# Dilated attention with one softmax for three mixed heads, and experts' further blocks one in a pass

## The reference

```python
for g, (window, r) in enumerate(A_GROUPS):          # (128, 1), (512, 4), (2048, 16)
    o, lse = banded_attention(gather(q), gather(k), gather(v), window // r)
    ...
alpha = jax.nn.softmax(jnp.stack(lses, axis=0), axis=0)
o = jnp.concatenate([outs[g] * alpha[g][..., None] for g in range(3)], axis=2)
return o.reshape(B, T, A_WIDTH) @ w_o
```

## Time and profile before

| | |
|---|---|
| median of 3 runs | 3214.95 us (3212.82 to 3242.93) |
| profiled execution | 3215.8 us, of which the traced span is 3214.1 |
| TensorE busy | 2949.3 us (92%) |
| VectorE busy | 1804.9 us (56%) |
| ScalarE busy | 1418.2 us (44%) |
| GpSimd busy | 537.0 us (17%) |
| DMA | 455.57 MB, mean 142 GB/s |

### The profile page before, as it was taken

How to read it: one execution, slowest core, us unless ns; L and a number is a source line. 1 busy time by engine, 2 the same in 40 slices (tenths; PEclk the granted TensorE clock), 3 DMA queues, 4 the chain that set the end, 5 groups by cost and what they waited for, 6 DMA issues and landing times. The chain is left out here.

```text
span 3214.1 us, 36964 instructions
## 1 busy us (share of the span) xinstructions
PE 2949.3 (92%) x14442; PEld 2357.6 (73%) x14442; DVE 1804.9 (56%) x2210; ACT 1418.2 (44%) x1885; POOL 537.0 (17%) x706
## 2 busy tenths in 40 slices
PE   7978899898998799999999789889999899889998
PEld 4856788787886487777777368678887697678887
DVE  4447745436544498888886344655543327455543
ACT  3324526336223188888786123443332325333332
POOL 0005414124101522232232100000000104000000
PEclk9989999898999799999999889899999999999999
DMA  5210101022652299999997730323322301223331
GB/s 198 60 54 1 60 27 53 27 53 75 213 184 110 96 353 363 364 365 372 375 375 297 280 116 1 92 67 104 106 92 79 95 27 53 73 77 95 92 104 41
DMA packets 277404, 455.57 MB, mean 142 GB/s; under 512 B 24656, under 2 KB 206800, under 8 KB 258160
## 3 DMA queue, kind: packets, MB, share of 16 engines
q1 hardware_dynamic: 250832, 398.43, 35.6%
q0 software_dynamic: 26400, 54.79, 4.7%
HBM read 450.77 MB, written 39.08 MB: 152 GB/s over the span
## 5 line engine op out<-in xcount | busy, mean ns | idle before, releaser
L253 DVE TENSOR_TENSOR weight_part<-weights,weight_part 128x2048 fp32r<-128x2048 f32 (+1 forms) x65 | 148.1, 2279 | 161.7 <-ACT weight_part L242 161.7
L1005 ACT ACTIVATE up_room<-banks,tap_columns 128x512 f32<-128x512 f32 x88 | 68.6, 779 | 315.4 <-PE banks L298 315.4
L293 PE MATMUL banks<-hT_r,weight_part 128*128 128x512 f32 x496 | 200.4, 404 | 4.6 <-PEq L846 2.9
L1046 DVE SCALAR_TENSOR_TENSOR up_room<-banks,tap_columns,up_room 128x511 f32<-128x511 f32 x88 | 66.0, 749 | 240.0 <-ACT up_room L1005 240.0
L242 ACT ACTIVATE weight_part<-weights 128x2048 fp32r<-128x2048 f32 (+1 forms) x65 | 121.7, 1872 | 176.3 <-PE banks L293 170.5
L298 PE MATMUL banks<-hT_r,weight_part 128*128 128x512 f32 x496 | 195.8, 395 | 0.0
L671 POOL TENSOR_SCALAR branch_mean<-branch_mean 128x1 f32<-128x1 f32 x20 | 4.4, 222 | 1129.7 <-ACT up_room L665 750.1
L293 PE MATMUL banks<-hT_r,weight_part_o 128*128 128x512 f32 x432 | 174.7, 404 | 7.1 <-PEq L110 4.2
L253 DVE TENSOR_TENSOR weight_part_o<-weights,weight_part_o 128x2048 fp32r<-128x2048 f32 (+2 forms) x49 | 106.9, 2181 | 127.0 <-ACT weight_part_o L242 127.0
L298 PE MATMUL banks<-hT_r,weight_part_o 128*128 128x512 f32 x432 | 170.9, 396 | 0.0
L297 PE MATMUL banks<-h_low,weight_part_o 128*128 128x512 f32 x432 | 169.8, 393 | 0.0
(11 more groups left out here) (723 smaller groups left out, 8834.9 us busy)
## 6 DMA issues: line engine op xcount, KB each, us to landing
weights<-in_w_e_gate SPq DMA_DIRECT2D x44, 1024.0 KB, 15.8
weights<-in_w_e_up SPq DMA_DIRECT2D x44, 1024.0 KB, 10.8
hT<-in_w_e_down SPq DMA_DIRECT2D x44, 1024.0 KB, 16.9
weights<-in_w_up SPq DMA_DIRECT2D x88, 512.0 KB, 5.1
gate_up<-in_w_e_gate SPq DMA_DIRECT2D x22, 1024.0 KB, 15.7
gate_up<-in_w_e_up SPq DMA_DIRECT2D x22, 1024.0 KB
down<-in_w_e_down SPq DMA_DIRECT2D x22, 1024.0 KB
weights<-in_w_down SPq DMA_DIRECT2D x20, 1024.0 KB, 5.0
```

Source lines behind the costliest of these rows:

```text
L253: c.nc.vector.tensor_tensor(low[:, 0:z], self.raw[n % RAW_SLOTS][:, 0:z], high[:, 0:z].bitcast(F32), ALU.subtract).then_inc(self.low_ready, 1)
L293: ins = c.nc.tensor.matmul(out, lhs[0], rhs[0], start=start, stop=False)
L1005: nc.scalar.activation(a[:, f % 2, v], c.ps[:, 2 * (f % 4) + v], ACT.Identity, scale=conv[:, 2, ch:ch + 1], bias=bias[:, ch:ch + 1]).then_ ...
L1046: nc.vector.scalar_tensor_tensor(a[:, f % 2, v, 1:], c.ps[:, 2 * (f % 4) + v, 0:SEQ - 1], conv[:, 1, ch:ch + 1], a[:, f % 2, v, 1:], ALU.m ...
```

## The change

**Attention and mixing become one stage.** Heads hd, hd + 4 and hd + 8 are mixed with each other. A softmax in each and a mixing by the log-denominators is the same as one softmax over all their scores together, 512 + 128 + 128 = 768 columns, with one maximum and one sum. `dilated_attention(c, triples, pair, tiles)` goes through 16 triples (4 query blocks x 4 heads). The shares are now scaled by one over the sum before they are turned (VectorE, two new instructions), and in the values product v stands (64 columns) while the turned shares move (128 columns), so that the result is already turned: features x tokens. Two triples fill a bank of 3 x 128 columns, the even head in partitions 0 to 63, the odd one in 64 to 127; ScalarE and VectorE take it out as high and low parts of the projection's operand. ScalarE, not VectorE, copies the turned shares. There is one room for turned shares in the banks, where there were two. `dilated_out` is gone; the asking for w_o's weights stands at the start of the stage, the split of the first tile in the middle of it. The mask is one table of 4 x 768 columns (1.5 MB) instead of 4 x 512 and 2 x 128.

```diff
-            for i in range(U + 3):
+            for i in range(J + 3):
+                if i < J:
+                    if i >= 2:
+                        pe.wait_ge(masked, i - 1)
+                    for at, w, q, k in triples[i]["scores"]:
+                        last = nc.tensor.matmul(scores(i)[:, at:at + w], q, k, start=True, stop=True)
+                    last.then_inc(scored, 1)
+                if 0 <= i - 3 < J:
+                    j = i - 3
+                    n = j // 2
+                    pe.wait_ge(copied, j + 1)
+                    if j % 2 == 0 and n >= 2:
+                        pe.wait_ge(lows, n - 1)
+                    for g, (p0, values) in enumerate(triples[j]["values"]):
+                        for x, (b, v) in enumerate(values):
+                            last = nc.tensor.matmul(c.ps[p0:p0 + DH, 6 + n % 2, g * P:(g + 1) * P], v, prT[:, j % 2, b * P:(b + 1) * P],
+                                                    start=x == 0, stop=x == len(values) - 1)
+                    last.then_inc(summed, 1)
+                if 0 <= i - 2 < J:
+                    j = i - 2
+                    pe.wait_ge(scaled, j + 1)
+                    if j >= 1:
+                        pe.wait_ge(copied, j)
+                    for b in range(KA):
+                        last = nc.tensor.transpose(turned_bank()[:, b * P:(b + 1) * P], pr[:, j % 3, b * P:(b + 1) * P], c.ident[:])
+                    last.then_inc(turned, 1)
...
         @block.scalar
+            for i in range(J + 4):
+                if i < J:
+                    act.wait_ge(biased, i + 1)
+                    nc.scalar.activation(pr[:, i % 3], pr[:, i % 3], ACT.Exp, bias=nm[:, i % 3:i % 3 + 1],
+                                         scale=DH ** -0.5, accum_out=total[:, i % 3:i % 3 + 1]).then_inc(expd, 1)
+                if 0 <= i - 2 < J:
+                    j = i - 2
+                    act.wait_ge(turned, j + 1)
+                    if j >= 2:
+                        act.wait_ge(summed, j - 1)
+                    nc.scalar.activation(prT[:, j % 2], turned_bank(), ACT.Copy).then_inc(copied, 1)
+                if 0 <= i - 4 < J and (i - 4) % 2:
+                    n = (i - 4) // 2
+                    act.wait_ge(summed, i - 3)
+                    nc.scalar.activation(dst(0, n), drained(n), ACT.Copy).then_inc(highs, 1)
+                if i == J // 2:
+                    c.split.high_ahead(c, act)
...
         @block.vector
+            for i in range(J + 4):
+                if i < J:
+                    z = slice(i % 3, i % 3 + 1)
                     dve.wait_ge(scored, i + 1)
                     if i >= 3:
                         dve.wait_ge(turned, i - 2)
                         dve.wait_ge(expd, i - 2)
+                    nc.vector.tensor_tensor_reduce(pr[:, i % 3], scores(i), triples[i]["mask"], 1.0, 4 * NEG, ALU.add, ALU.max, top[:, z]).then_inc(masked, 1)
+                    dve.wait_ge(masked, i + 1)
+                    nc.vector.tensor_scalar(nm[:, z], top[:, z], -DH ** -0.5, None, ALU.mult).then_inc(biased, 1)
+                if 0 <= i - 1 < J:
+                    j = i - 1
+                    z = slice(j % 3, j % 3 + 1)
+                    dve.wait_ge(expd, j + 1)
+                    if j >= 3:
+                        dve.wait_ge(scaled, j - 2)
+                    nc.vector.reciprocal(share[:, z], total[:, z]).then_inc(shared, 1)
+                    dve.wait_ge(shared, j + 1)
+                    nc.vector.tensor_scalar(pr[:, j % 3], pr[:, j % 3], share[:, z], None, ALU.mult).then_inc(scaled, 1)
+                if 0 <= i - 4 < J and (i - 4) % 2:
+                    n = (i - 4) // 2
+                    dve.wait_ge(highs, n + 1)
+                    nc.vector.tensor_tensor(dst(1, n), drained(n), dst(0, n).bitcast(F32), ALU.subtract).then_inc(lows, 1)
+                if i == J // 2:
+                    c.split.low_ahead(c, dve)
```

```diff
-            with sp.Fori(0, n, 2) as i:
...
+            with sp.Fori(0, n, 1) as i:
+                e = weights(i)
+                sp.wait_ge(l_up_done, i + 1)
                 sp.sem_inc(passed, 1)
+                later_gate_up(e)
+                sp.wait_ge(l_down_done, i + 1)
                 sp.sem_inc(passed, 1)
+                later_down(e)
...
-            with pe.Fori(0, n, 2) as i:
...
+            with pe.Fori(0, n, 1) as i:
+                pe.wait_ge(l_x_left, i + 1)
+                pe.wait_ge(l_x_right, i + 1)
+                pe.wait_ge(l_gu_in, 32 * i + 32)
+                pe.wait_ge(l_gated, i + 1)
+                for k in range(KD):
+                    last = nc.tensor.matmul(c.ps[:, 0], x_all[0][:, k], gu[lset][:, :, k], start=k == 0, stop=k == KD - 1)
+                last.then_inc(l_up_done, 1)
+                pe.wait_ge(l_gated, i + 2)
+                pe.wait_ge(l_copied, i + 1)
+                turn_hid(0).then_inc(l_turned, 1)
+                pe.wait_ge(l_copied, i + 2)
+                pe.wait_ge(l_down_in, 16 * i + 16)
+                pe.wait_ge(l_y_ready, i + 1)
+                for hf in range(2):
+                    for k in range(2):
+                        last = nc.tensor.matmul(c.ps[:, 3 + hf], hid_all[0][:, k], wd[lset][:, k, hf * GW:(hf + 1) * GW], start=k == 0, stop=k == 1)
+                last.then_inc(l_down_done, 1)
+                pe.wait_ge(l_gathered, 16 * i + 32)
+                turn_x(0).then_inc(l_x_turned, 1)
...
-            L(V.tensor_scalar(even[:, 0:TABLE // 2], iota[0:1, 0:TABLE:2], nrow[:, 0:1], None, ALU.is_lt))
-            L(V.tensor_reduce(nrow[:, 1:2], even[:, 0:TABLE // 2], AX, ALU.add))
-            L(V.tensor_scalar(nrow[:, 2:3], nrow[:, 1:2], 1.0, 2.0, ALU.max, ALU.mult))
+            L(V.tensor_scalar(nrow[:, 2:3], nrow[:, 0:1], 1.0, None, ALU.max))
```

More of the change, by code:

```diff
@@ L360, with dilated_attention @@
 FT = 256
-def attention(c, units):
+def dilated_attention(c, triples, pair, tiles):
     nc = c.nc
-    U = len(units)
+    J = len(triples)
     with ExitStack() as s:
-        pr = c.sb(s, "probs", [P, 3, SEQ])
-        prT = c.sb(s, "probsT", [P, 2, NT, P])
+        room = c.over(c.hT, "joint_room", [P, KD * SEQ], F32)
+        pr = room[:, 0:3 * A_W].rearrange("p (i n) -> p i n", i=3)
+        prT = c.over(c.hT, "joint_turned", [P, 2, A_W], F32, 3 * A_W)
+        top = c.sb(s, "maxima", [P, 3])
@@ L373, in attention @@
         nm = c.sb(s, "minus_max", [P, 3])
[L374 to L381 removed]
+        total = c.sb(s, "sums", [P, 3])
+        share = c.sb(s, "shares", [P, 3])
+        scored = c.sem("jt_scored")
+        masked = c.sem("jt_masked")
+        biased = c.sem("jt_biased")
@@ L1476, in block2 @@
         with ExitStack() as s:
-            o = c.sb(s, "heads_out", [P, NT, A_W])
-            m = c.sb(s, "maxima", [P, NT, A_HEADS])
-            l = c.sb(s, "sums", [P, NT, A_HEADS])
+            plain = c.sb(s, "oT_parts", [P, 2, KA, SEQ])
+            rounded = c.rounded(plain)
+            pair = [rounded[:, x] for x in range(2)]
+            w = t["w_o_a_2"][0]
+            groups = [(0, 2), (2, 4)]
             with ExitStack() as sa:
@@ L1499, in masks @@
                     row(sp, rows[:, 1], gains[0, 2:3], landed)
[L1500 removed]
+                    sp.wait_ge(landed, 16 * 4)
                 jobs = []
@@ L1513, in block2 @@
                                        rhs=lambda w, h, k: w[:, k * FT:(k + 1) * FT]) for tile in range(NT)]))
-                project_heads(c, jobs, None, given=h, tables=(tables, roping, 32), late=masks)
-                units = []
+                project_heads(c, jobs, None, given=h, tables=(tables, roping, 32), late=masks, scratch=plain[:, 0, 0:3])
+                triples = []
                 for cc in range(4):
-                    for hd in range(A_HEADS):
+                    own = slice(cc * P, (cc + 1) * P)
+                    for hd in range(4):
                         p0 = DH * (hd % 2)
-                        g = hd // 4
-                        keys = slice(0, SEQ) if g == 0 else slice(cc * P, (cc + 1) * P)
-                        units.append(dict(
-                            W=SEQ if g == 0 else P, q=qT[p0:p0 + DH, hd // 2, cc * P:(cc + 1) * P], k=kT[p0:p0 + DH, hd // 2, keys],
-                            adds=[(c.ident[:], band[:, cc] if g == 0 else mask[:, g - 1], 0)],
-                            v=[v[:, b, hd * DH:(hd + 1) * DH] for b in (range(NT) if g == 0 else [cc])],
-                            out=o[:, cc, hd * DH:(hd + 1) * DH], m=m[:, cc, hd:hd + 1], l=l[:, cc, hd:hd + 1]))
-                attention(c, units)
-            pair = [c.sb(s, f"oT_{x}", [P, KA, SEQ], F32R) for x in ("high", "low")]
-            w = t["w_o_a_2"][0]
-            groups = [(0, 2), (2, 4)]
-            with ExitStack() as b:
-                dilated_out(c, b, o, m, l, pair, group_tiles(w, groups))
+                        wide, near, far = [(qT[p0:p0 + DH, x // 2, own], kT[p0:p0 + DH, x // 2]) for x in (hd, hd + 4, hd + 8)]
```

(15 more changed lines are left out.)

366 lines of the change are left out of this document (104 added, 262 removed).

## The result

The changed kernel takes 3198.5 us (median of 16 executions, 3194.6 to 3206.6); the kernel before, in 16 executions beside it, 3217.0 (3207.5 to 3247.1). The ratio is 0.9923, 95% interval 0.9898 to 0.9947: some 24 us, or 0.8%, less, where 12.4 were forecast. The two medians are only 18.5 us apart (0.9943); the means are 23.6 apart (0.9927), and the ratio lies near to theirs: it counts the longer executions of before too. Ratios in this document leave out executions more than 1.5% above the shortest of the same kernel; there are none in these two sets.

A forecast was written before the change was run, and what follows sets the result against it. TensorE was taken to set the old attention pace, with mixing a serial chain. 3215.8 - 12.7 (attention) - 0.7 (projection) + 0.9 (further blocks) = 3203.3, less 0.85 to the median: 3202.5 us, range 3193 to 3215.

The forecast's parts named there:

- The cover of the sum: Last step, whole kernel: the profiled execution is 0.85 us above the median of three runs, so 3203.3 becomes 3202.5.
- Attention stage: Attention and mixing, first score matmul to the projection's first matmul: 72.0 us instead of 84.7, a gain of 12.7.
- the chain of a pair: Attention loop: high, low, maximum, exp, copies, values and transposes close a chain of 8.13 us for two triples.
- The split in the middle: Attention loop: splitting the first weight tile at i == 8 in both queues adds 2.3 us.
- TensorE's work: Attention loop, one triple: scores 1.50, values 1.44, transposes 0.70, sum 3.64 us; 58 for 16 triples.
- Rival (c): Attention loop: the high-low chain is not closed, TensorE sets the pace; stage 66 us, kernel 3197; chance 0.11.
- Rival (a): Attention values: stationary loads of 64 columns are not hidden; 5.20 us a triple, +6 instead of -12.7, 3221 us; chance 0.10.
- change of form: TensorE in attention: 64-row score followed by 128-row transpose costs 0.20 us, other changes 0.04 to 0.06; new one taken as 0.12.
- Projection: Output projection behind attention: its first seven matmuls may escape the low clock; between 0 and -1.4 us, taken as -0.7.
- Further blocks: Experts' loop, one block a pass: second load waits for the first product; result at 1787.7, +0.9 us, from -1.5 to +6.
- rival (b): Experts' further blocks: the second pass costs a jump and register reads, as does SyncE's issue; +6 more, 3208.5 us; chance 0.13.
- Untouched stages: Sign of error, stages without code changes: the forecast is wrong if one moves by more than 2 us.

The follow-up runs named there:

- full_again: The whole change run again beside its two halves, attention part alone and further blocks alone: 3197.6 us, ratio 0.9911 to the kernel before.
- warm_experts: The whole change with TensorE's idle stretches in the experts' further blocks filled by identity products into an unused bank: 3197.9 us, ratio 0.991.
- a_only: Only the attention part of the change, with the experts' loop as in the kernel before: 3196.8 us, ratio 0.9908.
- the reordered kernels: New attention stage with VectorE's low part behind the next maximum, and the weight split moved to the drain: stage 66.6, then 65.86 us.

## Why the prediction was wrong

**The cover of the sum.** The step that failed is the first line of the sum: "The profiled execution is 0.85 above the median of the three runs shown". One profile, with the full clock all through the attention loop, stood for the kernel before. Of the three times shown one was 3242.93 us, 28 above the others, and it was given no cause and no term. The runs show what stands behind such times: the stage under change, at the low clock (28.2 us in the one long execution with a profile). The change takes 15.5 us from the shorter executions of before, where 12.4 were forecast, and some 9 us more by ending the longer ones (the mean of the 16 is 3222.9, the median of the shorter ten 3214.0); neither the forecast nor a rival had a case for these. Without them, 3202.5 was 4 us off the measured 3198.5, in the range. Part of that was luck: between the two profiles the attention stage gave 3.6 us more than forecast, the projection and what lies behind it 2.1 and all that lies ahead of the further blocks 3.8, and the further blocks 3.1 less, with 0.7 lost behind them.

**Attention stage, 72.0 forecast, 68.4 measured.** The mechanism was right, its size was off. First high after 18.1 us (18.9 forecast), seventh high 46.6 later (49.3), the rest 3.7 (3.8). The mis-sized term is the chain of a pair, 8.13 us: 7.68 measured. (The split in the middle cost 1.8, not 2.3; the end without scores gave 1.2, not 1.8.) I had laid recorded durations end to end; on one engine the next instruction starts before the recorded end of the last (low 0.86 long, the maximum 0.78 behind it; a copy 0.81 long, the high 0.71 behind it). TensorE's work was forecast as 3.64 and is 3.75: the transposes take 0.80 and not 0.70. Rival (c), the chain not closed at 66 us, was wrong for this kernel; that its 3197 lies near to the measured 3198.5 is chance. With the chain opened the stage took 66.6, and 65.9 with the split moved too.

**Rival (a)** is out: the value records start 0.109 us apart, and take 0.121 each with the change of form in it, where 0.11 and 0.12 for the change were forecast. Their weights take 137 ns to load (group by form, TensorE's loads):

```profile
L422 PEld LDWEIGHTS banks<-joint_turned_o,v 128*64 128x64 f32 x192 | 20.5, 137 | 8.1 <-ACT joint_turned_o L446 7.3
```

So that load is hidden. The rule of the Trainium skill's page "TensorE: Matmul & The Clock Gate", The mechanism, under which a load with the same row group is not, doesn't hold for them.

The prediction read the old loop as if one change of form cost 0.20 us and the others almost nothing. The starts say otherwise: at each change, either way, the first gap is 0.20 us instead of 0.11. With the wider gap beside it a group of scores, of values and of transposes in the new loop takes 0.20, 0.14 and 0.15 us more than its records, 0.49 for a triple; forecast were 0.37. The page "TensorEngine Tiling (Array Packing)" of the Trainium skill, Key Properties, says that each change of tiling mode drains the engine; priced at 0.20 each, as in the prediction, that is 0.60. The trace lies in the middle. That the stage came out at 68.4 and not at 73.8 doesn't tell against the rule: the chain's overlaps made that difference.

**Projection, -0.7 forecast, 0 measured.** In the profile of after the clock fell at 2048.5 us, within 0.4 us of the first matmul, and seven steps of 0.43 follow, where before had one of 0.56 and six of 0.43; its first tile took 7.2 us in both. It fell there in `full_again` and `warm_experts` too, but not in `a_only`, with the same loop, nor in the reordered kernels. So both bounds occur, and -0.7 lay between them.

**Further blocks, +0.9 forecast, +2.7 in the mean of the profiles, +4.0 in the one of after.** SyncE issued 0.26 us after the product's end (so rival (b), a costly second pass, is out). The second product started 9.0 us after the end of the first, 8.2 forecast, and the first one 8.1 us after the 63rd's down product, 9.1 forecast; these two errors cancel. What I missed is that the clock falls in the waits left between the steps, for 1.7 us a product; with it kept the forecast would have been right (37.3 us, 37.5 forecast).

**Untouched stages** moved by up to 3.8 us between the two profiles (the end of the expert loop came that much earlier, the stretch behind the attention stage was 2.8 shorter), by which test I called myself wrong. The clock had more time at the low level in the profile of before (a mean of 0.960 over the span, after 0.965), and the test was too narrow for that.

## What to carry to other kernels

Look at every single time of the kernel before, not at the median and one profile: a group of executions some per cent longer is a state of some stage, and a change that touches that stage is worth its share too. A loop of small matmuls in which TensorE is hardly idle can still lose the clock; fewer and wider matmuls shortened this loop, and none of 67 executions lost it. Lay out a chain by differences of starts, not by durations, and put an operation that nobody waits for behind the one that somebody does.

## What was not expected of the hardware

- The granted clock fell to 1.2 GHz in a stretch in which TensorE's records leave hardly a gap (27.0 of 28.0 us busy ahead of it), with scores of 64 rows and value products of 64 moving columns; and once low it stayed low for 68.3 us, though each group then took 1.7 to 1.8 times as long and TensorE was busy 60.00 of 60.00 us. With one matmul of full height and 128 columns more for each group, eleven of twelve executions lay within 9 us.
- Where TensorE goes from one form of matmul to another, the next record starts 0.20 us later instead of 0.11, and the gap beside it is wider too: six scores take 1.50 us to the values' start, and their records only 1.30 (4 x 0.11 + 2 x 0.43).
- A stage at the full clock repeats to 0.05 us (68.42, 68.43, 68.44 and 68.44 in four profiles, the old one 84.69, 84.69 and 84.74), while the whole program scatters over 4 to 12 us.
